# First attention: the maximum of the next step is taken ahead of scaling the probabilities of the step in front of it

## The reference, cut to what matters

```python
def block(q):
    s = jnp.einsum('bqkgd,bnkd->bkgqn', q, keys).astype(jnp.float32) * scale
    p = jax.nn.softmax(s, axis=-1)
    return jnp.einsum('bkgqn,bnkd->bqkgd', p.astype(vals.dtype), vals)
```

## Time and profile before

| What | Value |
|---|---|
| Median of 3 runs | 972.46 us (971.69 to 974.57) |
| The profiled execution | 974.37 us |
| Span of its trace | 971.4 us |
| Mean granted TensorE clock | 0.941 of full |
| TensorE matmul busy | 881.0 us (91%) |
| VectorE busy | 424.2 us (44%) |
| ScalarE busy | 419.3 us (43%) |
| GpSimd busy | 413.1 us (43%) |

### The profile page before, as it was taken

One profiled execution on the slowest core, in us unless ns is written; L12 is line 12 of the kernel. 1 busy time (PEld: TensorE's weight loads), 2 busy tenths in 40 slices (PEclk: granted clock), 3 DMA queues, 4 the chain that ended last, 5 costly groups with the idle time before them and its releaser, 6 DMA issues.

```text
span 971.4 us, 14105 instructions
## 1 busy us (share of the span) xinstructions
PE 881.0 (91%) x5427; PEld 740.6 (76%) x5427; DVE 424.2 (44%) x641; ACT 419.3 (43%) x648; POOL 413.1 (43%) x199
## 2 busy tenths in 40 slices
PE   4999896979999699999997799999998599999995
PEld 3678775865547589999996688778796489999994
DVE  3554464893250633232334425453317643344334
ACT  4344212124534434344444464554474444544442
POOL 2434000000015246657463688443384455665652
PEclk9999987989959899999999699999999789999998
DMA  9773744115613245566653377333254236565541
GB/s 311 239 247 90 251 149 142 45 44 174 173 36 116 87 136 182 184 192 185 198 177 100 131 203 184 110 93 102 88 153 135 81 119 203 176 192 176 193 151 44
DMA packets 93531, 145.52 MB, mean 150 GB/s; under 512 B 15403, under 2 KB 63760, under 8 KB 93488
## 3 DMA queue, kind: packets, MB, share of 16 engines
q1 hardware_dynamic: 92608, 143.23, 47.4%
q0 software_dynamic: 848, 1.70, 0.6%
q10 hardware_dynamic: 32, 0.01, 0.0%
HBM read 143.87 MB, written 1.05 MB: 149 GB/s over the span
## 4 chain that ended last, share of the span: by engine, by line
PE 75%; DVE 12%; issue 5%; ACT 4%; POOL 2%; DMA 2%; SPq 0%; DVEq 0%; ACTq 0%; POOLq 0%
PE bank L1525 73%; ACT w_hi L647 1%; DMA raw<-in_w_mod 1%; PE bank L1779 1%; POOL w_lo L592 1%; DVE h_f L1123 1%; POOL z_lo L621 1%; PE bank L2068 1%; DMA raw<-in_w_in 1%; DVE yn L1489 1%; DVE merged_lo L1476 1%; DVE x L1495 0%; DVE hg_kb L1216 0%; DVE hg_kf L1216 0%; DVE hg_at L1227 0%
## 5 line engine op out<-in xcount | busy, mean ns | idle before, releaser
L592 POOL TENSOR_TENSOR w_lo<-raw,w_hi 128x1024 fp32r<-128x1024 f32 (+2 forms) x163 | 392.6, 2422 | 521.0 <-ACT w_hi L647 499.8
L647 ACT ACTIVATE w_hi<-raw 128x1024 fp32r<-128x1024 f32 (+1 forms) x218 | 226.9, 1044 | 238.9 <-PE bank L1525 199.4
L1061 DVE TENSOR_TENSOR w_lo<-raw,w_hi 128x1024 fp32r<-128x1024 f32 x58 | 74.5, 1294 | 138.1 <-ACT w_hi L647 137.9
L1525 PE MATMUL bank<-z_hi,w_hi 128*128 128x256 f32 x384 | 111.8, 291 | 2.4 <-POOL z_lo L621 2.4
L1525 PE MATMUL bank<-z_lo,w_hi 128*128 128x256 f32 x384 | 110.3, 287 | 0.0
L1525 PE MATMUL bank<-z_hi,w_lo 128*128 128x256 f32 x384 | 110.2, 287 | 0.0
L1525 PE MATMUL bank<-n_hi,w_hi 128*128 128x256 f32 x352 | 100.2, 285 | 1.4 <-DVE w_lo L1061 0.5
L1525 PE MATMUL bank<-n_lo,w_hi 128*128 128x256 f32 x352 | 98.9, 281 | 0.0
L1525 PE MATMUL bank<-n_hi,w_lo 128*128 128x256 f32 x352 | 98.8, 281 | 0.0
L1525 PE MATMUL bank<-w_hi,mlp_h_hi 128*128 128x512 f32 x216 | 84.9, 393 | 2.9 <-DVE mlp_h_lo L1511 1.5
L1525 PE MATMUL bank<-w_lo,mlp_h_hi 128*128 128x512 f32 x216 | 84.7, 392 | 0.0
(11 more groups left out here) (361 smaller groups left out, 1674.8 us busy)
## 6 DMA issues: line engine op xcount, KB each, us to landing
raw<-in_w_in SPq DMA_DIRECT2D x54, 512.0 KB, 4.6
raw<-in_w_down SPq DMA_DIRECT2D x54, 512.0 KB, 3.7
raw<-in_w_gu SPq DMA_DIRECT2D x44, 512.0 KB, 3.5
raw<-in_w_mod SPq DMA_DIRECT2D x32, 512.0 KB, 4.2
raw<-in_w_up SPq DMA_DIRECT2D x32, 512.0 KB, 3.7
raw<-in_w_mod SPq DMA_DIRECT2D x32, 256.0 KB, 6.2
raw<-in_w_out SPq DMA_DIRECT2D x12, 512.0 KB, 3.5
raw<-in_w_in SPq DMA_DIRECT2D x8, 336.0 KB, 2.9
```

Source lines behind the costliest of these rows:

```text
L592: nc.gpsimd.tensor_tensor(wl[:, w % SPL, 0:size], raw[:, slot_raw, 0:size], wh[:, w % SPL, 0:size].bitcast(F32), ALU.subtract).then_inc(s_ ...
L647: nc.scalar.activation(wh[:, w % SPL, 0:size], raw[:, slot_raw, 0:size], ACT.Copy).then_inc(s_hi, 1)
L1061: V.tensor_tensor(wl[:, w % SPL, :], raw[:, slot_raw, :], wh[:, w % SPL, :].bitcast(F32), ALU.subtract).then_inc(s_lod, 1)
L1525: return nc.tensor.matmul(out_, l, r_, start=start, stop=stop, skip_group_check=True)
```

## The change

VectorE's call of `probs(n - 1)` is moved from the head of step n to behind `max n`. No instruction is added or removed, and no other engine's list changes. The order on VectorE becomes `m 0, max 0, m 1, max 1, probs 0, m 2, max 2, probs 1`, and so on. At n = 11 `hg_out` now follows `probs(10)` and stands ahead of `m 12`, `max 12` and `probs(11)`.

```diff
             for n in range(16):
-                if n >= 1:
-                    probs(n - 1)
                 dve.wait_ge(PE.sem, PE[f"scores {n}"])
                 done(V.tensor_reduce(stat[:, 128 + n:129 + n], ps[n % 2][:], AX, ALU.max), f"m {n}")
                 done(V.tensor_scalar(stat[:, 128 + n:129 + n], stat[:, 128 + n:129 + n], -HD ** -0.5, None, ALU.mult), f"max {n}")
+                if n >= 1:
+                    probs(n - 1)
                 if n == 11:
                     hg_out()
                 if n == 10:
```

## The result

The changed kernel took 985.0 us as the median of 4 runs (981.2 to 986.3), the kernel before 972.92 us (971.69 to 974.57, 4 runs). The ratio is 1.0115, with a 95% interval of 1.0086 to 1.0143; applied to 972.92 it gives 984.1 us. The change makes the kernel about 1.15% slower. The direction and most of the mechanism were as forecast; the size is 11 to 12 us where 8.1 had been forecast.

What follows compares the result with a forecast made beforehand. The prediction took TensorE's list to bound the stage; exposed waits of 1.76 + 0.80 + 1.52 + 3.52 = 7.60 us plus 0.5 for the clock gave +8.1, 980.6 us against the median 972.46. The 8-in-10 range was 976.5 to 984.5.

Steps and rivals of the forecast that it cites:

- What bounds the stage: Stage of the change: mostly TensorE's own list; VectorE's 24.9 us and ScalarE's 17.0 us of waits don't end last.
- The price of the gap: From the end of the scores to the transposes, through maximum and scaling: 1.76 us where TensorE has no other work.
- The covers: TensorE's work between scores n+1 and step n's transposes; steps 0 to 5 expose nothing, the shortest being 2.02 us.
- Step 7's 0.80: At step 7 one mean product covers 0.96 of the gap, leaving +0.80 us exposed.
- Step 8's: Another 0.80 us exposed at step 8, hidden in TensorE's idle 1.64 us before step 9's transposes: 0.
- Steps 10 and 11, 1.52: Around `hg_out`: it starts 0.60 later and `m 12`, `max 12` follow it, so step 11's transposes come 1.52 us later.
- Steps 12 and 13, 3.52: No TensorE work between scores and transposes there: +1.76 us at each step, 3.52 together.
- 14 and 15 nothing: Steps 14 and 15: `gate 1` gives TensorE 5.4 us of other work, so 0 is added.
- The gain side, 0: Earlier exponentials at steps 1, 2, 9, 10, 12: 0 to 3.0 us gain, taken as 0; rival 969.5 us, 4%.
- the shift is passed on in full after 300 us: Behind the stage no wait was found that would swallow a later start, so the whole delay reaches the end.
- The clock, +0.5: `scores 12` wholly at the half clock costs 0.6 more, 0.5 of it added; ends -1.5 and +3.9.
- the second rival: Clock drops behind step 6's wait, +2.3, and `gate 1` runs wholly at half clock, +1.5: 983.9 us, 15%.

Runs made afterwards that it cites:

- e1_covered: Kernel before, with the scaling moved behind the maximum only at n = 1 to 6, 10 and 15: 973.75 us, ratio 1.000.
- e14_fill: Changed kernel plus a useless TensorE product in the waits at steps 6, 10, 11, 12 and 13: 978.8 us, ratio 1.0043 against the kernel before.
- e3_step6: Kernel before, with the new order at n = 7 alone, so only step 6's transposes wait: 977.02 us, ratio 1.0037.
- e5_hg_path: Kernel before, with the new order only at n = 11 and 12, around `hg_out`: 976.43 us, ratio 1.0037.
- e4_last_two: Kernel before, with the new order only at n = 13 and 14: 977.59 us, ratio 1.0045.
- e13_hg_split: Kernel before, with only the two bank-reading products of `hg_out` left at n = 11, its other three instructions after `probs(15)`: 969.65 us, ratio 0.9965.
- e11_double_max_new: Changed kernel with every maximum over 512 scores taken twice: 994.1 us, against the changed kernel's 985.0.
- e8_hgout14: Kernel before, with `hg_out` moved from n = 11 to n = 14: 973.68 us, ratio 1.0006.
- e10_covered_hgout14: Kernel before, with `hg_out` at n = 14 and the new order only at n = 1 to 6, 10 and 15: 974.93 us, ratio 1.001.

## Why the prediction was right, and where it was short

- What bounds the stage, and that ScalarE's and VectorE's waits are worth nothing there: right. VectorE's wait for `exp` fell by 24 us and the kernel became slower; `e1_covered` moved eight scalings and gained nothing.
- The price of the gap, 1.76 us from five rows: right (30.87 to 32.63 at step 6; about 1.7 of shown idle time each). The covers were right as well: 0.26 us to spare was enough at step 1, whose transposes come 3.66 us after the first ones in both kernels.
- Step 7's 0.80: right (0.64 shown, about 0.8 from the end of the product). Step 8's, hidden in TensorE's 1.64 us before step 9: right; that wait shrank to 0.56.
- Steps 10 and 11, 1.52: the sum came out, the path did not. The prediction had TensorE's path and that of `hg_out` equal at 278.6 and took the wait of step 10 as hidden beside `hg_out`. In the trace `scores 12` ran wholly at the half level and ended after `hg_out`, so `hg_out` is off the path and both gaps are paid. Less the wait of before they come to 1.57, next to the 1.52, and `scores 12` took 0.70 longer; together that is the 2.28 measured (6.41 less 4.13). That the number came out follows from two paths that were forecast as equally long, and is in part luck.
- Steps 12 and 13, 3.52, and 14 and 15 nothing: right.
- The gain side, 0: right, shown by `e1_covered` for three of the five steps; for n = 9 and 12 it is only not contradicted.
- That the shift is passed on in full after 300 us: right, 7.9 against 8.0.
- The clock, +0.5: too small; this is the term that was mis-sized. It is 1.96 us in the profiled execution. Over all executions it is some 4 (11.2 to 12.1 less 7.6); the three without a trace had a lower mean clock, and where theirs fell is not known. The +0.5 stood for the half clock of `scores 12` alone, which measured 0.70. What it left out is above all the fall behind step 6, 1.52 us. That was the first half of the second rival, which had 15%, 2.3 us for it and 983.9 in all. Its second half, a gate wholly at the half level, did not come (4.7 us of the gate's 5.98 at the half level, against 3.9 of 5.47). So the result lies near that rival's time, but its mechanism is seen only in part. I took the half clock of steps 10 to 13 as given and its ends as chance. `e14_fill` speaks for its being itself an effect of the waits: put work in them, and most of it goes.
- The rule of the Trainium skill ("TensorE: Matmul & The Clock Gate", "A second HAM failure mode: psum-queue depth-cycling"), that repeated short idle times cost more than themselves through the clock: the runs agree, with 6 to 7 us between the changed kernel and `e14_fill`. They add that one wait can be enough, 3.40 us for 1.76 in the trace of `e3_step6`.

## What to carry to other kernels

Before an instruction is moved ahead of another in an engine's list, list what the other engine does between the two things that it will now have to wait for in turn; where that is nothing, the whole latency of the inserted work shows, however idle both engines look. An order is not right or wrong for a loop but for a step: the same two instructions, moved, cost nothing that could be seen at nine steps and 11 us at six. And look for waits of 1.5 to 2 us on TensorE. Here they cost about twice themselves in `e3_step6` and `e5_hg_path`, and no more than themselves in the trace of `e4_last_two`; taking one away (in `e13_hg_split` by splitting off what is not needed yet) brought about twice the wait.

## What the runs showed of the hardware that was not expected

- Useless work can pay: five products in the waits, of 0.91 us each at the full clock, took 6 to 7 us off.
- Behind one wait of 1.76 us, between scores and transposes at step 6, the granted clock fell from 1.00 to 0.50 (`e3_step6`), while the same stretch without it stayed at 1.00 in the kernel before. Behind a wait of 2.42 us in the same place it stayed at 1.00 (`e11_double_max_new`). What decides between the two is open. Executions of the same kernel differ too: the spans of the changed kernel with twice the maximum run from 987.8 us at a mean clock of 0.935 to 997.4 at 0.922.
- The half level can last under a TensorE that is busy throughout: in the kernel before it was busy, by its records, for all of the 13.7 us from 276.8 us on, and the granted clock was 0.50.
- A cast on VectorE took four times as long beside work on GpSimd. In `e8_hgout14` the cast into `cat_hi` took 2.72 us while GpSimd's subtraction ran from 283.38 to 285.84, and the same in `e10_covered_hgout14` beside such a subtraction; in the other twelve traces, where none ran beside it, it took 0.69:

```profile
283.67 2.72 DVE L1289 CAST cat_hi<-xn 128x1024 fp32r<-128x1024 f32 x1
```

That GpSimd is the cause is read from the overlap alone and was not tested.
